# Starts of SBUF buffers at multiples of 64 bytes, in a float32 transformer kernel on one Trainium2 core

## The reference, cut to what matters

```python
h = rms_norm(x, norm_g[l])
z = h @ w_in[l]                    # 2048 columns in, 7168 and more out
...
x = x + y @ w_out[l]
```

## The kernel before

| buffer | start before | mod 64 | mod 256 |
|---|---|---|---|
| con | 8320 | 0 | 128 |
| xr (hi; lo is 16512 further) | 44000 | 32 | 224 |
| pairs (the weights, in steps of 512) | 99616 | 32 | 32 |
| parts0 (first output projection) | 195904 | 0 | 64 |
| parts2, parts4 (feed-forward) | 137504 | 32 | 32 |
| yr | 196576 | 32 | 224 |

## Time and profile before

### The profile page before, as it was taken

One profiled execution on the slowest core, in us unless ns is written; L12 is line 12 of the kernel. 1 busy time (PEld: TensorE's weight loads), 2 busy tenths in 40 slices (PEclk: granted clock), 3 DMA queues, 4 the chain that ended last, 5 costly groups with the idle time before them and its releaser, 6 DMA issues.

```text
span 3807.3 us, 66928 instructions
## 1 busy us (share of the span) xinstructions
PE 3609.8 (95%) x29212; PEld 3540.2 (93%) x29212; DVE 2329.7 (61%) x3649; ACT 1603.7 (42%) x2257; POOL 123.4 (3%) x97
## 2 busy tenths in 40 slices
PE   7999999999979998899999999968998999999997
PEld 7899999999978897899999999968998989999997
DVE  4655555555665787686556555677556866566455
ACT  4444444443544321255444444452334554444333
POOL 0000000000000000010000000001000100000001
PEclk9999999999989998899999999989999999999998
DMA  6445455544443320155555555532443545555563
GB/s 220 149 164 163 166 178 173 185 164 161 161 137 115 100 75 29 67 175 169 189 182 183 188 180 184 170 112 78 133 145 107 176 167 189 187 178 188 182 183 122
DMA packets 162630, 587.99 MB, mean 154 GB/s; under 512 B 18144, under 2 KB 18144, under 8 KB 161952
## 3 DMA queue, kind: packets, MB, share of 16 engines
q1 hardware_dynamic: 160848, 575.06, 45.9%
q0 software_dynamic: 1488, 8.65, 0.7%
HBM read 581.54 MB, written 2.10 MB: 153 GB/s over the span
## 4 chain that ended last, share of the span: by engine, by line
PE 56%; DVE 6%; POOL 1%; ACT 1%; issue 1%; DMA 0%; POOLq 0%; ACTq 0%; DVEq 0%
PE bank L1816 16%; PE bank L1817 16%; PE bank L1818 16%; PE bank L1986 1%; PE bank L1977 1%; DVE pairs L2534 1%; POOL xs L3139 1%; PE bank L1995 1%; DVE right L2960 1%; PE bank L1830 0%; PE bank L1832 0%; PE bank L1831 0%; PE bank L2028 0%; ACT pairs L2229 0%; ACT xs L2280 0%
## 5 line engine op out<-in xcount | busy, mean ns | idle before, releaser
L1816 PE MATMUL bank<-xr,pairs 128*128 128x256 f32 (+1 forms) x5664 | 1630.8, 288 | 92.5 <-DVE xr L2538 47.8
L2229 ACT ACTIVATE pairs<-raw 128x1024 fp32r<-128x1024 f32 x1108 | 1144.8, 1042 | 1084.5 <-PE bank L1818 975.5
L1817 PE MATMUL bank<-xr,pairs 128*128 128x256 f32 (+1 forms) x5664 | 1600.2, 283 | 0.0
L1818 PE MATMUL bank<-xr,pairs 128*128 128x256 f32 (+1 forms) x5664 | 1598.1, 282 | 0.0
L2534 DVE TENSOR_TENSOR pairs<-raw,pairs 128x1024 fp32r<-128x1024 f32 x1108 | 1320.3, 1211 | 381.9 <-ACT pairs L2229 380.4
L1816 PEld LDWEIGHTS bank<-xr,pairs 128*128 128x128 f32 x5664 | 1078.5, 190 | 108.4 <-DVE pairs L2534 49.8
L1817 PEld LDWEIGHTS bank<-xr,pairs 128*128 128x128 f32 x5664 | 1080.7, 191 | 1.9
L1818 PEld LDWEIGHTS bank<-xr,pairs 128*128 128x128 f32 x5664 | 1077.9, 190 | 0.0
L1816 PE MATMUL bank<-parts,pairs 128*128 128x256 f32 x1792 | 508.6, 284 | 3.6 <-DVE parts L2538 3.3
L1817 PE MATMUL bank<-parts,pairs 128*128 128x256 f32 x1792 | 506.5, 283 | 0.0
L1818 PE MATMUL bank<-parts,pairs 128*128 128x256 f32 x1792 | 506.1, 282 | 0.0
(11 more groups left out here) (558 smaller groups left out, 3581.8 us busy)
## 6 DMA issues: line engine op xcount, KB each, us to landing
raw<-in_w_in SPq DMA_DIRECT2D x176, 512.0 KB, 4.3
raw<-in_gate SPq DMA_DIRECT2D x176, 512.0 KB, 4.4
raw<-in_val SPq DMA_DIRECT2D x176, 512.0 KB, 4.1
raw<-in_down SPq DMA_DIRECT2D x160, 512.0 KB, 4.3
raw<-in_l_w_in SPq DMA_DIRECT2D x146, 512.0 KB, 3.6
raw<-in_w_out SPq DMA_DIRECT2D x64, 512.0 KB, 4.4
raw<-in_l_w_out SPq DMA_DIRECT2D x64, 512.0 KB, 4.0
raw<-in_v_in SPq DMA_DIRECT2D x48, 512.0 KB, 4.6
```

The costliest lines, as they stand in the source:

```text
L1816: mm(o, wh[:, qs], rh[:, k, :], start=begin and q == 0, stop=False)
L1817: mm(o, wh[:, qs], rl[:, k, :], start=False, stop=False)
L1818: last = mm(o, wl[:, qs], rh[:, k, :], start=False, stop=end and q == c - 1)
L2229: e.activation(pair_of(n)[0], raw_of(n), ACT.Copy).then_inc(*hi_made(n))
```

## The change

Every buffer and every piece of an arena gets a start at a multiple of 64 bytes (16 columns of float32). The rows of xr move from 258 to 272 columns apart, while the views that are read stay 256 or 258 wide. Sizes are padded, the arenas and the far side get a few columns more or less, and room is made by halving the reserve for POOL's DMA descriptors from 8192 to 4096 bytes. A small buffer of 32 bytes, `edge`, moves the far side down by 32 bytes. No instruction is added, removed or moved in any engine's order; `con` and `vec` are fetched with 15 and 5 columns more.

```diff
@@ -33,6 +33,8 @@
 XW = T + 2
+LINE = 16
+XS = T + LINE
@@ -59,7 +61,7 @@
-NVEC = _n
+NVEC = -(-_n // LINE) * LINE
@@ -72,7 +74,7 @@
-NCON = _n
+NCON = -(-_n // LINE) * LINE
@@ -308,6 +310,11 @@
+def whole(cols):
+
+    return -(-cols // LINE) * LINE
+
+
@@ -327,10 +334,11 @@
-    xr = sb("xr", 2 * KT * XW, F32R)
-    nbuf = sb("nbuf", 6 * T + 12)
+    xr = sb("xr", 2 * KT * XS, F32R)
+    nbuf = sb("nbuf", 6 * T + 16)
...
+    ctx.enter_context(nc.sbuf_tensor("edge", [128, 8], F32, side="right"))
@@ -371,7 +379,7 @@
-    XG = v3(xr[:, 0:KT * XW], KT), v3(xr[:, KT * XW:], KT)
+    XG = tuple(v3(xr[:, i * KT * XS:(i + 1) * KT * XS], KT)[:, :, 0:XW] for i in range(2))
@@ -392,7 +400,7 @@
         o = mark[side]
-        mark[side] += cols
+        mark[side] += whole(cols)
@@ -1785,13 +1793,13 @@
-            mempart = phase(19700 - 7920, 2 * KT * T, True)
+            mempart = phase(11840, 2 * KT * T, True)
...
-            cpart, cpart2 = phase(9032, 1536, True, 1024, 8192)
+            cpart, cpart2 = phase(9120, 1536, True, 1024, 8256)
...
-            phase(7944, 0, True, 0, 11712)
+            phase(7952, 0, True, 0, 11840)
@@ -3368,7 +3376,7 @@
-    nc = bacc.Bacc("TRN2", target_bir_lowering=False, num_devices=1, dynamic_dma_scratch_size=8192)
+    nc = bacc.Bacc("TRN2", target_bir_lowering=False, num_devices=1, dynamic_dma_scratch_size=4096)
```

## The result

The changed kernel takes **3819.99 us** (median of 13 executions, 3811.24 to 3822.05), the kernel before in the same session 3809.32 (13, 3806.2 to 3816.33). The ratio is 1.0023, 95% interval 1.0015 to 1.0032: slower by about 9 us (the two medians lie 10.7 apart), where 20 us less was forecast. The profiled execution after took 3819.99 us, that of before 3809.18: 10.8 us between them.

What follows compares the result with a forecast made beforehand. TensorE's matmuls were taken to set the pace. x -29.7, yr +10.0, parts0 +2.6, `row` -3.4 and feed-forward 0 summed to -20.5 us, from 3811.4 to 3790.9 us, with a whole range of 3718 to 3843.

Steps and rivals of the forecast that it cites:

- Feed-forward, 0 us: Feed-forward's 4224 matmuls: both sides move to 64 mod 256, the distance stays 0, so no change.
- yr, +10.0: yr's 1536 matmuls: distance 192 becomes 128, from 113.3 to 120 ns each, +10.0 us.
- row 8 of x: Row of x before the change, hi at distance 0 and lo at 128, 120 ns; taken to show 128 costs what 0 costs.
- parts0, +2.6: First output projection, 1152 matmuls: distance 32 becomes 0, +2.3 ns each, +2.6 us.
- x, -29.7: x's 16992 matmuls: four distances 192, 0, 64, 128 average 117.2 ns, -1.8 ns each, -29.7 us.
- The expected pattern of two rows near 0.34 and two near 0.36 us: Sign in the timeline after: x's rows in a pattern of four, two near 0.34 us and two at 0.36.
- The upper end that I gave for this term: x's mean if distance 64 costs 120 ns: 118.3 ns a matmul, a gain of only 0.7 ns.
- `row`, -3.4: The 1920 `row` products, same distances with sides exchanged: the same -1.8 ns each as x, -3.4 us.
- The lower end of the range: 3718 us, given as two thirds of the way down to the 3674 of the rival that the start itself counts.
- The slow rival: All buffers lock at the slow 120.0 ns, x +1.0 ns a matmul: +31 us, 3842 us; chance 0.28, wholly or halfway.
- The rule of distances: A matmul's cost follows the bytes from weights' start to moving row's start, mod 256; basis of the -20.5 us, chance 0.41.
- Edits costed at nothing: VectorE and ScalarE durations, fetches, extra `con` columns and the halved descriptor reserve: no cost; a `con` wait bounded at 10 us.

Runs made afterwards that it cites:

- e1: The changed kernel with feed-forward, parts and yr moved to distance 192 from the weights, x left as changed: 3777.73 us, ratio 0.9908 to the kernel before.
- m1: Matmuls only, 108 bursts without pauses, both sides at chosen places, no other engine beside them: 113.3 to 120.0 ns a matmul at fixed distances.
- e5: e4 with xr alone 64 bytes further on, so every row of x stands at distance 0: 3828.37 us, ratio 1.0050 to the kernel before.
- e6: e4 with the parts and feed-forward buffers at distance 192 too: 3712.62 us, ratio 0.9756 to the kernel before.
- e4: The kernel before with x's rows 320 columns apart, all at distance 192, descriptor reserve 1024 bytes: 3753.09 us, ratio 0.9862.
- e12: e6 with the moving buffers (x, parts, yr) shifted to distance 112, weights left in place: 3709.36 us, ratio 0.9733 to the kernel before.
- m2: Matmuls only, 256 bursts of 48, hi and lo each at distances of their own: two pairs take 113.3 ns, the mean of all is 118.1.
- e7: e4 profiled once more, nothing changed: 3740.36 us.
- m4: Matmuls only, 288 bursts with a pause before each, sixteen moving starts, three weights' starts, six restarts each: at distance 112, 113.5 or 120.0 ns by weights' start.
- e10: e6 with the weights moved 80 bytes on, putting the moving sides at distance 112: 3828.85 us, ratio 1.0054 to the kernel before.

## Why the prediction was wrong, by its own steps

1. **Feed-forward, 0 us:** right. 1669 matmuls in 200 us, as the earlier trace rows; and e1 moved it by distance alone, to 113.3.
2. **yr, +10.0:** right in its sign, +8.5 in the profiled pair. By row 8 of x I took distance 128 to cost 120; fixed, it is 118.6 in m1, and in the kernel 118.7 in one mixer and 119.8 in the other. The row was a poor witness: two of its three matmuls move hi, at distance 0, and one moves lo, at 128.
3. **parts0, +2.6:** right, +2.9.
4. **x, -29.7: the step that failed.** Measured -11.3, 0.7 ns a matmul instead of 1.8. Three things in it were off. Distance 64, which no row showed, is 117.8 and not 115.6. I put it nearer its mirror 192 on a symmetry that the map does not have. 128 was 1.4 ns too dear. These two nearly cancel: the mean of the four would be 117.4 instead of 117.2. What remains is that I took a mean over rows at all: with the distance changing from row to row, m1 has 118.3 to 118.5, the kernel 118.3. The expected pattern of two rows near 0.34 and two near 0.36 us isn't there either; the rows of after take 353 to 358 ns each. The means came from streams that keep one distance for hundreds of matmuls, x never keeps one for more than three, a difference that I passed over. The upper end that I gave for this term, 118.3, was the value, by luck: I had it from distance 64 at 120.
5. **`row`, -3.4:** measured -0.2. I gave these products x's -1.8 ns without reading what they took: 118.6 ns before, and 118.4 after. Their four distances after are the same set as x's, and they end up beside x's 118.3; they had started below its 119.0.

With these sizes (and +0.3 of other matmuls) the sum is +0.2 in place of -20.5, no change of time. The lower end of the range has a slip too, which changes nothing: two thirds of the way from 3811 to 3674 is 3720, not 3718. The slow rival, which I had at 0.28, gave the right side on a wrong ground: it has x at 120.0, and x got faster.

**The term that was missing** is the clock. I read 0.974 in one execution and used it as a constant. The same kernel shows 0.970 to 0.975, and 3805 to 3821 us with it; after is in the lower group more often, which put 10.9 us into the profiled pair. Nothing of this could be read from one profile, but the spread of the runs shown, 3809 to 3816, was a hint of a size that I set at nothing. The 0.2% that I called the least that can be told from no change was about what came out.

**What held.** That one shape has different costs by its place, which vanish at half clock, was the right reading of the earlier trace rows. The rule of the Trainium skill weighed there, "SBUF — State Buffer", section "SBUF: two separate sides", by which TensorE's two reads wait for nobody, does not describe these runs: with no other engine at work 113.3 and 120.0 ns stand side by side in m1. By that rule e5 and e6 would take the same time; they are 116 us apart. That it is the two reads that collide is an argument from the dependence on both starts, and not shown by a counter. The rule of distances itself held while both sides moved by 32 bytes, and failed in three ways that only later runs showed: two cadences at one distance, the weights' start mod 32, and another cadence for 258 columns.

**Edits costed at nothing** cost nothing that shows: VectorE's 2328.9 us against 2329.7, ScalarE's 1603.6 against 1603.7, and the descriptor reserve, which e4 cut to an eighth and e12 to a sixteenth with the time going down.

## What to carry to other kernels

Where TensorE is bound by matmuls that each load their own weights, compare the start-to-start time of equal matmuls on different buffers at full clock: if they differ, make every row of the moving side stand at one and the same good distance from the weights (row step a multiple of 256 bytes), found by a map of bursts, rather than align to a round number; the alignment here left the feed-forward at the dear distance 0, where it was, and moved parts0 there. Map it with a pause before each burst and several restarts, since one burst shows only one of two cadences, with the weights where the kernel has them mod 32 and with the kernel's own widths, and prefer a place that shows one. Before a change of some tenths of a per cent is explained, sort the executions by granted clock and take a second profile of the unchanged kernel.

## What was not expected of the hardware

- fp32r matmuls of 128x128 by 128x256 with their own LDWEIGHTS take 113.3 to 120.0 ns at full clock by the place of both operands mod 256 bytes (one pair of m2 121.3); at half clock 213.2 and 213.5 at the two places read the earlier trace rows.
- A place can have two cadences, 113.3 or 117.8 ns at 192. Which of them follows a pause differs from execution to execution, and it holds for thousands of matmuls (3840 at 117.8 in e4, 3840 at 113.3 in e6 and e7), worth 17 us in one stretch.
- (112, 112) and (192, 192) alone of m2's 256 pairs of distances for hi and lo showed 113.3 ns, 272 cycles of 2.4 GHz for 256 columns. With restarts it turned up at others too: at 16 once and at 144 twice of six with the weights at a multiple of 32, at 64 six times of twelve with them at 16 mod 32 (m4).
- The weights' start at 16 mod 32 turns distance 112 from the best into nearly the worst (e12 and e10, 119 us apart); at 192 with the weights at 16 mod 32 all twelve restarts took 113.3.
- 258 columns at a place where 256 take 113.3 take 119.4 (e12).
- Time follows the mean granted clock from one execution to the next: 3809 us at 0.973 and 0.974, 3818 at 0.970 and 0.971, same kernel, with short half-clock stretches that come or stay away behind the same pauses.
